# A latent-attention stage with its transposes one step later, a fourth probability buffer, and its projections dealt out anew

## The reference

```python
def softmax_attention(q, k, v):
    s = jnp.einsum('bqhd,bkhd->bhqk', q, k).astype(jnp.float32) * ((QK_NOPE + QK_ROPE) ** -0.5)
    p = jax.nn.softmax(s, axis=-1)
    return jnp.einsum('bhqk,bkhd->bqhd', p.astype(v.dtype), v)

def mla_mixer(a_ctx, a_lat, w_in, q_norm_w, w_uq, kv_norm_w, w_ukv, w_out, rope, need_ctx):
    q_c, k_c, v_c = mla_project(a_ctx, w_in, q_norm_w, w_uq, kv_norm_w, w_ukv, None)
    q_l, k_l, v_l = mla_project(a_lat, w_in, q_norm_w, w_uq, kv_norm_w, w_ukv, rope)
    k_all = jnp.concatenate([k_c, k_l], axis=1)
    v_all = jnp.concatenate([v_c, v_l], axis=1)
    ...
    o_l = lax.map(lambda qb: softmax_attention(qb, k_all, v_all), q_blocks)
    out_l = jnp.moveaxis(o_l, 0, 1).reshape(b, l, MLA_WIDTH) @ w_out
```

## Time and profile before

| what | value |
|---|---|
| median of three runs | 2524.29 us |
| the profiled execution, its time | 2524.43 us |
| the profiled execution, its span | 2522.6 us |
| mean granted clock of TensorE in it | 0.982 |
| TensorE busy | 2378.9 us, 94% |
| VectorE busy | 1181.0 us, 47% |
| ScalarE busy | 744.3 us, 30% |
| GpSimd busy | 224.8 us, 9% |

### The profile page before, as it was taken

The page is one execution under the profiler, slowest core; times in us unless marked ns, Lnnn a source line. Parts: engine busy times, 40 slices in busy tenths (PEclk is TensorE's granted clock), DMA queues, the critical chain, the costliest instruction groups (busy, mean ns, idle before and its releaser), DMA issues.

```text
span 2522.6 us, 30573 instructions
## 1 busy us (share of the span) xinstructions
PE 2378.9 (94%) x12716; PEld 1741.5 (69%) x12716; DVE 1181.0 (47%) x1953; ACT 744.3 (30%) x1287; POOL 224.8 (9%) x207
## 2 busy tenths in 40 slices
PE   7998999999998998899999999999998888999998
PEld 6783463333344988647888888877777767788886
DVE  3247332111364677835443433444566573544444
ACT  2235111111132434314112111123555563322222
POOL 0000011111103106200000000000202031000000
PEclk9999999999999999899999999999999999999999
DMA  9947749898511211222112212212001011233221
GB/s 342 360 144 255 257 169 380 321 367 332 190 26 35 68 51 43 92 83 67 51 51 84 67 51 67 67 51 61 30 1 55 17 68 53 91 99 100 91 88 72
DMA packets 177961, 308.86 MB, mean 122 GB/s; under 512 B 18459, under 2 KB 85395, under 8 KB 177696
## 3 DMA queue, kind: packets, MB, share of 16 engines
q1 hardware_dynamic: 164720, 278.40, 31.8%
q0 software_dynamic: 12368, 26.35, 3.0%
q10 hardware_dynamic: 736, 2.15, 0.2%
HBM read 355.05 MB, written 18.93 MB: 148 GB/s over the span
## 4 chain that ended last, share of the span: by engine, by line
PE 59%; DVE 9%; ACT 4%; issue 1%; DMA 0%; POOL 0%; DVEq 0%; ACTq 0%
PE PS L140 37%; PE PS L2544 11%; PE PS L2482 2%; PE PS L152 2%; PE PS L3131 2%; DVE X L110 2%; DVE Rr L110 1%; PE PS L3052 1%; PE PS L2488 1%; DVE H L110 1%; ACT X L130 1%; PE PS L2420 1%; DVE MIX L110 1%; DVE gate L110 1%; DVE H L118 1%
## 5 line engine op out<-in xcount | busy, mean ns | idle before, releaser
L140 PE MATMUL PS<-at,wH 128*128 128x512 f32 (+1 forms) x2144 | 563.8, 352 | 2.1 <-DVE at L110 2.1
L140 PEld LDWEIGHTS PS<-at,wH 128*128 128x128 f32 x2144 | 378.8, 190 | 57.0 <-issue 1.6
L140 PE MATMUL PS<-at,rest 128*128 128x512 f32 (+1 forms) x1072 | 376.6, 351 | 0.0
L2544 PE MATMUL PS<-wH,ac 128*128 128x512 f32 x880 | 277.9, 393 | 3.3 <-DVE hn L110 3.3
L110 DVE TENSOR_TENSOR rest<-ring,wH 128x2048 fp32r<-128x2048 f32 x66 | 150.4, 2291 | 211.2 <-ACT wH L133 210.6
L140 PEld LDWEIGHTS PS<-at,rest 128*128 128x128 f32 x1072 | 202.9, 189 | 27.2
L133 ACT CAST wH<-ring 128x2048 fp32r<-128x2048 f32 x66 | 124.6, 1906 | 264.5 <-PE PS L2544 199.8
L2544 PEld LDWEIGHTS PS<-wH,ac 128*128 128x128 f32 x880 | 165.2, 188 | 43.0 <-DVE hn L110 8.5
L2544 PE MATMUL PS<-rest,ac 128*128 128x512 f32 x440 | 171.4, 389 | 0.0
L140 PE MATMUL PS<-HI,ATr 128*128 128x256 f32 x512 | 148.6, 290 | 5.2 <-DVE MIXr L110 4.7
L140 PE MATMUL PS<-ring,AT 128*128 128x512 f32 x320 | 141.7, 599 | 0.8 <-ACT AT L133 0.8
(11 more groups left out here) (386 smaller groups left out, 4162.7 us busy)
## 6 DMA issues: line engine op xcount, KB each, us to landing
R<-in_w_gate_up_dram SPq DMA_DIRECT2D x32, 1024.0 KB, 11.2
ring<-in_w_down_dram SPq DMA_DIRECT2D x32, 1024.0 KB, 12.9
ring<-in_w_gate_up_dram SPq DMA_DIRECT2D x32, 1024.0 KB
ring<-in_w_ffn_gate_dram SPq DMA_DIRECT2D x22, 1024.0 KB, 5.4
ring<-in_w_ffn_up_dram SPq DMA_DIRECT2D x22, 1024.0 KB, 5.4
ring<-in_w_ffn_down_dram SPq DMA_DIRECT2D x22, 1024.0 KB, 5.0
ring<-in_w_ada_dram SPq DMA_DIRECT2D x16, 1024.0 KB, 7.4
HIw<-in_w_gate_up_dram SPq DMA_DIRECT2D x16, 1024.0 KB, 8.5
```

Of the source, the lines that this page charges most:

```text
L140: ins = self.e.matmul(out, l, r, start=k == 0, stop=k == len(pairs) - 1)
L2544: ins = p.e.matmul(bk(4 + n_dn % 3), a_, b_, start=start and i == 0, stop=stop and i == len(terms) - 1)
```

## The change

- The transposes in loop n are those of unit n-3 instead of n-2, and so are the two copies to `pTm`; the loop runs to 67 instead of 66. The probabilities have four buffers, the fourth in `oT`'s place up to unit 35 and in `gate` from unit 39.
- A head's O comes in loop n = 7, 11, 15, ... instead of 6, 10, 14, ..., and stands between S and T instead of behind T.
- The tables deal some projections to a loop one later or one earlier: V at 36 to 38, QP at 24 and 25, and single entries of the others.
- In `latent_pool` the order of GpSimd's passes is pe 0, wq 0, pe 1, pe 2, wq 1, wq 2 instead of pe 0, wq 0, pe 1, wq 1, pe 2, wq 2.
- The DMA of gate 5 moves to the end of GpSimd's stage, behind the last transposes.

```diff
@@ -2928,9 +2928,12 @@
...
-        for j in range(3):
-            pe_low(g, 0, j)
-            wq_low(g, 0, j)
+        pe_low(g, 0, 0)
+        wq_low(g, 0, 0)
+        pe_low(g, 0, 1)
+        pe_low(g, 0, 2)
+        wq_low(g, 0, 1)
+        wq_low(g, 0, 2)
 
 
 
@@ -2938,7 +2941,8 @@
     vm = AT1[:, 0:3072].rearrange("p (t d) -> p t d", t=6)
...
-    pb = [X[:, 4608:5376], X[:, 5376:6144], R[:, 10240:11008]]
+    pbs = [X[:, 4608:5376], X[:, 5376:6144], R[:, 10240:11008], MIX1[:, 2048:2816], gate[:, 0:768]]
+    pb = lambda n: pbs[n % 4 + (n % 4 == 3 and n > 36)]
     pTm = AT1[:, 3072:6144].rearrange("p (b q) -> p b q", b=6)
...
@@ -2969,14 +2973,14 @@
...
-    V_AT = {0: (1, 2), 1: (3, 4), 2: (5,), 35: (6, 7), 36: (8, 9), 37: (10, 11)}
-    QP_AT = {23: (0, 1), 24: (2, 3)}
-    QN_AT = {2: 1, 8: 2, 17: 3, 26: 4, 32: 5, 41: 6, 49: 7}
-    KN_AT = {4: 1, 11: 2, 16: 3, 28: 4, 31: 5, 40: 6, 48: 7}
-    PT_AT = {5: 1, 13: 2, 19: 3, 29: 4, 34: 5, 44: 6, 52: 7}
+    V_AT = {0: (1, 2), 1: (3, 4), 2: (5,), 36: (6, 7), 37: (8, 9), 38: (10, 11)}
+    QP_AT = {24: (0, 1), 25: (2, 3)}
+    QN_AT = {2: 1, 8: 2, 17: 3, 26: 4, 33: 5, 41: 6, 49: 7}
+    KN_AT = {4: 1, 10: 2, 16: 3, 28: 4, 32: 5, 40: 6, 48: 7}
+    PT_AT = {5: 1, 13: 2, 20: 3, 29: 4, 35: 5, 44: 6, 52: 7}
     WP_AT, WQ_AT = {20: 0, 21: 1, 22: 2}, {23: 0, 24: 1, 25: 2}
-    OH_AT = {51: (0, 1), 53: (2, 3), 58: (4,), 59: (5,), 60: (6,), 66: (7,)}
-    WO_AT = {54: 0, 55: 0, 56: 1, 57: 1, 61: 2, 62: 2, 63: 3, 64: 3}
+    OH_AT = {51: (0, 1), 53: (2, 3), 58: (4,), 59: (5,), 60: (6,), 67: (7,)}
+    WO_AT = {54: 0, 55: 0, 56: 1, 57: 1, 62: 2, 63: 2, 64: 3, 65: 3}
...
@@ -3091,7 +3095,7 @@
         p.wait_ge(S("q_high"), 2)
         p.wait_ge(S("q_low"), 2)
         v_pe(p, 0)
-        for n in range(67):
+        for n in range(68):
             if n < 64:
                 h, t = units[n]
                 e = h % 2
@@ -3108,29 +3112,29 @@
...
-            if 2 <= n < 66:
-                x = pb[(n - 2) % 3]
-                p.wait_ge(S("prob2"), n - 1)
-                p.wait_ge(S("k_pe_low"), 2)
-                p.wait_ge(S("pT_act"), n - 2)
-                p.turns([(bk(4, 128, 128 * b), x[:, 128 * b:128 * b + 128]) for b in range(4)], ident, S("p2_T"))
-                p.wait_ge(S("pT_dve"), n - 2)
-                p.turns([(bk(5, 128, 128 * b), x[:, 512 + 128 * b:640 + 128 * b]) for b in range(2)], ident, S("p2_T"))
-            if n >= 3 and units[n - 3][1] == 3:
-                h = units[n - 3][0]
+            if n >= 4 and units[n - 4][1] == 3:
+                h = units[n - 4][0]
                 p.wait_ge(S("v_take"), 6 * (h // 8) + 6)
                 p.wait_ge(S("q_pe_copy"), count(p, "q_pe"))
                 p.wait_ge(S("k_high"), 2 * count(p, "k_nope"))
                 p.wait_ge(S("k_low"), 2 * count(p, "k_nope"))
                 p.wait_ge(S("q_pe_low"), 2)
-                p.wait_ge(S("pT_act"), n - 2)
-                p.wait_ge(S("pT_dve"), n - 2)
+                p.wait_ge(S("pT_act"), n - 3)
+                p.wait_ge(S("pT_dve"), n - 3)
                 p.wait_ge(S("o2_copy"), 2 * h)
                 for b in range(6):
                     for e in range(2):
                         ins = p.e.matmul(PS[64 * e:64 * e + 64, 512 * 6:512 * 6 + 256], vm[:, b, 64 * (h % 8):64 * (h % 8) + 64],
                                          pTm[:, b, 256 * e:256 * e + 256], start=b == 0, stop=b == 5)
                 p.up(ins, S("o2"))
+            if 3 <= n < 67:
+                x = pb(n - 3)
+                p.wait_ge(S("prob2"), n - 2)
+                p.wait_ge(S("k_pe_low"), 2)
+                p.wait_ge(S("pT_act"), n - 3)
+                p.turns([(bk(4, 128, 128 * b), x[:, 128 * b:128 * b + 128]) for b in range(4)], ident, S("p2_T"))
+                p.wait_ge(S("pT_dve"), n - 3)
+                p.turns([(bk(5, 128, 128 * b), x[:, 512 + 128 * b:640 + 128 * b]) for b in range(2)], ident, S("p2_T"))
             if n in V_AT:
                 taken(p)
                 p.wait_ge(S("o2_copy"), 2 * count(p, "o2"))
@@ -3193,20 +3197,20 @@
             a.cast(k2(0, e, 0)[PE_[e], :], PS[PE_[e], 2048:2816], inc=S("k_pe_high"))
             q_pe_split(0, e)
         v_take(0)
-        for n in range(67):
-            if 2 <= n < 66:
-                t = units[n - 2][1]
-                a.wait_ge(S("p2_T"), 2 * (n - 2) + 1)
-                a.wait_ge(S("o2"), units[n - 2][0])
+        for n in range(68):
+            if 3 <= n < 67:
+                t = units[n - 3][1]
+                a.wait_ge(S("p2_T"), 2 * (n - 3) + 1)
+                a.wait_ge(S("o2"), units[n - 3][0])
                 a.cast(pTm[:, 0:4, 128 * t:128 * t + 128], bk(4).rearrange("p (b q) -> p b q", b=4), inc=S("pT_act"))
             if n < 64:
-                x, (m, l) = pb[n % 3], ml(n)
+                x, (m, l) = pb(n), ml(n)
                 b = 2 * (n % 2)
                 a.wait_ge(S("top2"), n + 1)
-                a.wait_ge(S("p2_T"), 2 * (n - 2))
+                a.wait_ge(S("p2_T"), 2 * (n - 3))
                 a.fn(x, PS[:, 512 * b:512 * b + 768], ACT.Exp, inc=S("exp2"), bias=m, accum_out=l)
-            if n >= 3 and units[n - 3][1] == 3:
-                h = units[n - 3][0]
+            if n >= 4 and units[n - 4][1] == 3:
+                h = units[n - 4][0]
                 r0 = 64 * (h % 2)
                 a.wait_ge(S("o2"), h + 1)
                 a.wait_ge(S("q_nope"), 8 if h >= 12 else 0)
@@ -3243,7 +3247,7 @@
                 for k in OH_AT[n]:
                     a.cast(oH(k), oT[:, k, :], inc=S("o_high"))
             if n in WO_AT:
-                i, q = WO_AT[n], 2 * (n % 2) if WO_AT[n] < 2 else 2 * ((n + 1) % 2)
+                i, q = WO_AT[n], 2 * (n % 2)
                 high_part(a, MWO + i, q)
                 high_part(a, MWO + i, q + 1)
 
@@ -3276,22 +3280,22 @@
             v.wait_ge(S("k_pe_high"), e + 1)
             v.tt(k2(0, e, 1)[PE_[e], :], PS[PE_[e], 2048:2816], k2(0, e, 0)[PE_[e], :].bitcast(F32), ALU.subtract, inc=S("k_pe_low"))
             q_pe_split(0, e)
-        for n in range(67):
+        for n in range(68):
             if n < 64:
                 b = 2 * (n % 2)
                 v.wait_ge(S("score2"), n + 1)
                 v.wait_ge(S("exp2"), n - 7)
                 v.red(ml(n)[0], PS[:, 512 * b:512 * b + 768], ALU.max, neg=True, inc=S("top2"))
             if 1 <= n <= 64:
-                x, (m, l) = pb[(n - 1) % 3], ml(n - 1)
+                x, (m, l) = pb(n - 1), ml(n - 1)
                 v.wait_ge(S("exp2"), n)
                 v.recip(l, l)
                 v.settle()
                 v.ts(x, x, l, None, ALU.mult, inc=S("prob2"))
-            if 2 <= n < 66:
-                t = units[n - 2][1]
-                v.wait_ge(S("p2_T"), 2 * (n - 2) + 2)
-                v.wait_ge(S("o2"), units[n - 2][0])
+            if 3 <= n < 67:
+                t = units[n - 3][1]
+                v.wait_ge(S("p2_T"), 2 * (n - 3) + 2)
+                v.wait_ge(S("o2"), units[n - 3][0])
                 v.copy(pTm[:, 4:6, 128 * t:128 * t + 128], bk(5, 256).rearrange("p (b q) -> p b q", b=2), inc=S("pT_dve"))
             if n in QP_AT:
                 for t in QP_AT[n]:
@@ -3318,7 +3322,6 @@
         v_low(g, 1)
         g.wait_ge(S("v_m"), 12)
         gates_rows(g, 1, 2, 1)
-        gates_rows(g, 1, 5, 1)
 
         def rest_of(*ks):
             for k in ks:
@@ -3336,6 +3339,8 @@
         wo_low(2)
         rest_of(7)
         wo_low(3)
+        g.wait_ge(S("p2_T"), 128)
+        gates_rows(g, 1, 5, 1)
 
 
 ```

## The result

| what | before | after |
|---|---|---|
| median | 2524.52 us (15 runs, 2520.41 to 2527.16) | 2529.80 us (15 runs, 2523.18 to 2536.95) |
| ratio, 95% interval | | 1.0026 [1.0016, 1.0035] |
| profiled execution: time, span | 2524.43, 2522.6 us | 2526.36, 2524.5 us |
| mean granted clock in it | 0.982 | 0.984 |
| TensorE busy | 2378.9 us | 2373.4 us |

The change makes the kernel 5.3 us slower. That is inside the range of 2516 to 2531 us, but beyond the 0.2% that separate a difference from nothing: the forecast of "no change" was wrong, and the case on the slower side came. The profiled execution of the changed kernel is one of its quicker ones, 3.4 us under its median. Part of that it owes to code that the change leaves alone: ahead of the last k_pe products TensorE was busy for 1704.9 us before and 1699.0 us after, with the same 9203 products, at granted clocks of 0.98 and 0.99.

What follows compares the result with a forecast made beforehand. TensorE was taken to bound projection stretches, VectorE plain ones, with about 37 us of TensorE idle at stake. Terms -0.85 - 1.5 + 1.8 - 4.6 + 0.3 + 0.6 + 5.0 = +0.75 on 2524.29 gave 2525 us; range 2516 to 2531.

Steps and rivals of the forecast that it cites:

- the forecast of "no change": Whole kernel: losses and gains cancel within 5 us, 2525 us expected, own range 2520 to 2530; chance 0.45.
- the case on the slower side: Rival: seven TensorE waits of 2.1 to 2.8 us, each with a full-price clock fall: +7.7 us, 2532; chance 0.22.
- Transposes one step later, 0: Attention loop: last two transposes still wait for VectorE's copy behind the scaling, so the 12.5 us of waits mostly change name.
- The product one loop later: Product with v no longer fills VectorE's splitting after the q_pe transposes; seven TensorE waits of 2.1 to 2.8 us result.
- the seven: TensorE waits of 2.1 to 2.8 us behind q_pe transposes or, once, the products making v; three of them new.
- S16 to S26: From unit 16's scores to unit 26's: -4.6 us, mainly QP's shorter wait, two clock falls gone, loop 18's work spread.
- S26 to S56: From unit 26's scores to unit 56's: +0.3 us, new waits against one clock fall gone, spread loops and shrunken waits.
- the tail: End of the attention stage, one loop more, last head's product with v later: +0.6 us, range -1 to +3.
- S0 to S16: From unit 0's scores to unit 16's: +1.8 us, new waits of 2.3, 2.3 and 0.7 against 3.2 gone and 0.3 returned.
- GpSimd's order: Projections ahead of attention: `pe_low(2)` before `wq_low(1)` starts the first QP 0.85 us earlier; bounds 0 and -1.5.
- The DMA of gate 5, 0: `gates_rows(1, 5)` at GpSimd's end: 0, its reader comes tens of us later; 4.9 us if that cover were gone.
- The clock: Half-clock stretches of 3.4 us around attention: removed falls priced 1.5, 1.2, 1.5 and 1.5; five new at 1.0, +5.0.

## Why the forecast was wrong, step by step

*Transposes one step later, 0: right.* The comparison with PT placed right in both gives 0 within its uncertainty, and the waits of the last two transposes for the copy (1.04 and 2.00 us above) show the reason. The waits changed their name, as said.

*The product one loop later: right in what it does, and mostly in size.* The waits of about 2.3 us ahead of O in loops 7, 15 and 31 are there, 2.40, 2.16 and 2.40 us, out of 5.83 us from PT to copy where the sum had 5.6. The other four of the seven came out under what was worked out: 2.0 us in two parts behind PT 20, 44 and 52 (2.4 to 2.8 expected), 1.94 behind PT 35 (2.1 to 2.4). Moving PT alone gave back 17.5 us.

For the sum by stretch I take the falls out on both sides, at the 1.4 us that the regression gives for one (before: two in S16 to S26, one in S26 to S56, one in the tail; after: one in S0 to S16, one in S16 to S26, three in S26 to S56, counting the double one twice). The prediction's own numbers without its clock items stand beside them:

| stretch | forecast without falls | measured without falls |
|---|---|---|
| front, GpSimd's order | -0.85 | -0.86 |
| S0 to S16 | +1.8 | 5.37 - 1.4 = +4.0 |
| S16 to S26 | -4.6 + 2.7 = -1.9 | -3.59 + 1.4 = -2.2 |
| S26 to S56 | +0.3 + 1.5 = +1.8 | 4.87 - 2.8 = +2.1 |
| tail | +0.6 | -1.41 + 1.4 = 0 |
| sum | +1.45 | +3.0 |

The 15 runs at equal clock say +2.5 for the last line.

*S0 to S16: 2.2 us short.* I priced k_nope in loop 10 at 0.7 us for its own wait and did not ask who waits for its split: O of loop 11 does, 1.86 us. The run with that product moved shows the exchange behind it: the wait went, and VectorE's time came up again at 1870.82 and 1876.80. So the missing term is VectorE's time for these splits and not that one wait; with PT late the whole stretch is as long as before the change.

*S16 to S26 and S26 to S56: right to 0.3 us.* QP's wait went from 2.33 to 0.48 us (0.7 was expected), and the 1.88 us wait behind PT 19 became 0.99 and 1.04 behind PT 20. The row of QP:

```profile
1913.15 0.36 PE L140 MATMUL PS<-gater,Hr 128*128 128x256 f32 x1 [0.48 <-ACT MIXb L133]
```

*Tail: the steps right, the sum 0.6 off.* The last O starts 11.75 us behind S63, where 11.7 was worked out:

```profile
2077.94 1.31 PE L140 MATMUL PS<-Rr 128*128 128x512 f32 x6
...
2089.69 2.81 PE L3127 MATMUL PS<-ATb 128*64 128x256 f32 x24 [0.59 <-ACT ATb L133]
```

*GpSimd's order, -0.85: right,* 0.86 in the trace of the change and in the run with that edit alone. QP starts 0.10 us behind the pass it waits for, the first of its kind there (1788.84 and not 1791.3, since this whole execution came to the place 2.4 us earlier):

```profile
1786.63 1.52 PE L146 MATMUL PS<-sm,R 128*128 128x32 f32 x12 [1.15 <-ACT R L133]
1786.78 0.62 ACT L133 CAST gater<-ring 128x512 fp32r<-128x512 f32 x1
...
1787.47 1.27 POOL L110 TENSOR_TENSOR rest<-ring,gater 128x512 fp32r<-128x512 f32 x1 [4.21 <-ACT gater L133]
...
1788.84 0.55 PE L140 MATMUL PS<-gater,Hr 128*128 128x256 f32 x1 [0.69 <-issue]
```

*The DMA of gate 5, 0: right.* From the first output product to the end both traces have 431.2 us.

*The clock: the step that failed.* In the sum the clock stands four times: -1.5 for the first fall, -2.7 for two that go with QP's and PT's waits, -1.5 for the one at loop 36, and +5.0 for five new ones. Together that is -0.7 us. By the runs it is about +2.8 (5.3 less 2.5, with a standard error of 1.2). This difference of 3.5 us is most of the 4.5 by which the sum missed; the rest is in the waits, above all in S0 to S16. Two things were wrong in it. I took four falls away at 1.4 us on average and put five back at 1.0, though nothing in the rows makes a new fall cheaper than an old one; at one price five against four is +1.4, which is 2.1 of the 3.5 us. The other 1.4 us are the further fall per run that only the regression shows. And I tied each fall to one wait of over 2 us. The count came true in the trace, six lengths of 3.4 us where one left over and five new ones make six, but by luck, for the places did not. Even the trace before did not bear this out well: the fall that I gave to the wait of 2.12 us came 3.0 us behind it, at 2085.63, directly behind another wait of 1.56 us (2085.03). After the change, the first fall stayed, though the second wait ahead of it had shrunk from 1.55 to 0.69 us; two waits of 2.40 and one of 2.16 us passed without one; others came behind waits of 1.0 to 1.9 us. The Trainium skill (TensorE: Matmul & The Clock Gate, Part 1) says that the gate's phase is free-running against the kernel. The runs agree, the changed kernel alone having mean clocks of 0.979 to 0.985. I had quoted that rule and still counted falls one by one from a single execution.

So the mechanism of the waits was seen, their sum (+1.45 us) came to within 1.0 to 1.6 us of what they measured (2.5 to 3.0), and the verdict was lost in the clock. "Slower" had 0.22 on the ground that six of seven falls must come at near full price; waits of 2.5 us and two more falls were enough.

What I also did not do is turn the second step around. The same reasoning says that PT belongs into the loop ahead of O, and that this one table, and not the pipeline, is where the 17.5 us lie.

## What to carry to other kernels

When two engines pipeline over units and a long block of one covers an extra task of the other, the pair has to be moved together: here one table of seven numbers was worth 17.5 us (12.9 at equal clock), the deeper pipeline by itself nothing. A software pipeline one step deeper frees only what does not hang on an in-order queue elsewhere; look where the copy that frees the shared bank stands in its engine's queue, and move that too (22.3 us with the table's repair, 2507.5 us in the end). And before a gain is put down to a structure, give its side edits to the old kernel: here it was then as fast as the deeper pipeline with its PT put right.

## What the runs showed of the hardware

The spread of one kernel over its runs, 14 us for the changed kernel, goes with its mean granted clock: correlation -0.96, about 1.4 us for a stretch of 3.4 us at half clock. Much of it need not come from the place that was changed: ahead of it the same 9203 products kept TensorE busy for 1704.9 us in one trace and 1699.0 us in the other. Two kernels whose medians differ by less than 5 us should be compared at an equal clock as well, and the changed stage by TensorE's idle time in it.

A fall can't be assigned to a wait from one execution. Waits of 2.40 us in loop 7 and 2.16 us in loop 15 were followed by none, and in the same trace one stood behind waits of 0.99 and 1.04 us. In the run with k_nope moved a fall did follow a wait of 2.40 us, now in loop 15.

The profile names the last releaser it can see; "issue" ahead of an O was a semaphore wait in both cases that I followed (the copy that starts at 1874.20, `k_low`'s split behind 1858.38), so a wait under that name need not be overhead.
